# High weights against high and low input in one product of 512 columns, in 45 units of a two-block transformer kernel

## The reference

```
# first block, MLP
u = rms_norm(h, norm_mlp_pre)
f = square(relu(u @ w_mlp_in)) @ w_mlp_out            # 1024 -> 4096 -> 1024
# second block, peer_ffn: x is the normed state, 16384 experts, 8 heads, 16 picked per head
q = x @ w_query;  s1 = q[..., 0] . keys_1;  s2 = q[..., 1] . keys_2
v1, i1 = top_k(s1, 16);  v2, i2 = top_k(s2, 16)
top_score, pos = top_k(v1[:, None] + v2[None, :], 16)
gates = softmax(top_score)
act = gelu(x . expert_down[picked], approximate=False)
y = sum over picked of gates * act * expert_up[picked]
```

## Time and profile before

| | us |
|---|---|
| median of 3 runs | 1545.17 |
| lowest, highest | 1544.93, 1547.18 |
| the profiled execution, whole | 1545.45 |
| its span | 1543.6 |
| PE busy in it | 1505.9 (98%) |
| DVE, ACT, POOL busy | 1037.6, 840.9, 366.4 |

### The profile page before, as it was taken

The page is one execution under the profiler, slowest core; times in us unless marked ns, Lnnn a source line. Parts: engine busy times, 40 slices in busy tenths (PEclk is TensorE's granted clock), DMA queues, the critical chain, the costliest instruction groups (busy, mean ns, idle before and its releaser), DMA issues.

```text
span 1543.6 us, 29249 instructions
## 1 busy us (share of the span) xinstructions
PE 1505.9 (98%) x11442; PEld 1423.4 (92%) x11442; DVE 1037.6 (67%) x1813; ACT 840.9 (54%) x1648; POOL 366.4 (24%) x398
## 2 busy tenths in 40 slices
PE   7999999999889999999999999999999999999998
PEld 7888989999889999999999999999999888888887
DVE  5666666555679774687999957777774555555554
ACT  4576465444455544454444467777775544455544
POOL 1452430000437652403655520011112000000000
PEclk9999999999999999999999999999999999999999
DMA  6752555555435622455455554444445555555664
GB/s 207 229 174 90 164 169 182 186 182 184 133 107 165 194 97 96 132 184 173 146 173 170 176 192 137 140 144 141 137 139 177 194 196 195 192 191 193 195 195 139
DMA packets 76805, 255.15 MB, mean 165 GB/s; under 512 B 9359, under 2 KB 15325, under 8 KB 76541
## 3 DMA queue, kind: packets, MB, share of 16 engines
q1 hardware_dynamic: 76429, 252.63, 50.3%
q0 software_dynamic: 240, 0.66, 0.2%
HBM read 250.23 MB, written 2.75 MB: 164 GB/s over the span
## 4 chain that ended last, share of the span: by engine, by line
PE 83%; DVE 11%; ACT 2%; POOL 1%; issue 1%; DMA 1%; SPq 1%; POOLq 0%; DVEq 0%; ACTq 0%
PE bank L684 82%; DVE wl L1701 3%; DVE big L1701 2%; POOL big L2419 1%; DVE big L2262 1%; DMA raw<-in_wst 1%; DVE big L2273 1%; DVE big L1704 1%; DVE big L2269 1%; ACT big L1266 1%; ACT wh L1266 1%; DVE big L2258 1%; DVE big L2279 1%; DVE big L2266 1%; PE bank L1015 0%
## 5 line engine op out<-in xcount | busy, mean ns | idle before, releaser
L1701 DVE TENSOR_TENSOR wl<-raw,wh 128x1024 fp32r<-128x1024 f32 (+4 forms) x467 | 542.4, 1163 | 377.8 <-ACT wh L1266 377.4
L1266 ACT ACTIVATE wh<-raw 128x1024 fp32r<-128x1024 f32 (+1 forms) x467 | 489.7, 1052 | 317.6 <-PE bank L684 310.0
L684 PE MATMUL bank<-gw,wh 128*128 128x256 f32 x3504 | 647.2, 286 | 0.0
L684 PEld LDWEIGHTS bank<-gw,wh 128*128 128x128 f32 x3504 | 544.7, 192 | 0.2
L684 PE MATMUL bank<-gw,wl 128*128 128x256 f32 x1752 | 495.9, 283 | 5.1 <-POOL wl L2419 5.1
L684 PEld LDWEIGHTS bank<-gw,wl 128*128 128x128 f32 x1752 | 335.2, 191 | 6.5 <-issue 6.5
L684 PE MATMUL bank<-xw,wh 128*128 128x256 f32 x1696 | 324.0, 291 | 12.7 <-ACT wh L1266 8.2
L684 PE MATMUL bank<-wh,xw 128*128 128x512 f32 x1056 | 325.2, 389 | 0.0
L684 PEld LDWEIGHTS bank<-xw,wh 128*128 128x128 f32 x1696 | 269.2, 195 | 20.0 <-ACT wh L1266 8.5
L2419 POOL TENSOR_TENSOR wl<-raw,wh 128x384 fp32r<-128x384 f32 (+5 forms) x140 | 194.8, 1399 | 304.6 <-ACT wh L1266 304.6
L1266 ACT ACTIVATE big<-bank 128x256 f32<-128x256 f32 (+23 forms) x327 | 118.2, 372 | 251.1 <-PE bank L684 214.4
(11 more groups left out here) (141 smaller groups left out, 1115.5 us busy)
## 6 DMA issues: line engine op xcount, KB each, us to landing
raw<-in_wst SPq DMA_DIRECT2D x455, 512.0 KB, 3.7
big<-toeplitz SPq DMA_DIRECT2D x16, 128.0 KB, 5.6
raw<-in_w1k SPq DMA_DIRECT2D x4, 512.0 KB, 5.4
raw<-in_w1v SPq DMA_DIRECT2D x4, 512.0 KB, 4.0
big<-in_xT SPq DMA_DIRECT2D x4, 256.0 KB, 5.8
raw<-in_wst SPq DMA_DIRECT2D x4, 256.0 KB, 5.0
diag_in<-big SPq DMA_DIRECT2D x2, 512.0 KB, 3.4
big<-in_keys SPq DMA_DIRECT2D x1, 1024.0 KB, 5.4
```

The source lines that it names most:

```text
L684: return e.matmul(o, a, b, start=first, stop=last, skip_group_check=True)
L1266: return e.activation(o, x, f, **kw)
L1701: return e.tensor_tensor(o, a, b, f)
```

## The change

45 units (`WIDE`) are computed in another way: the 30 "in" units of the MLP from 59 on, and the 15 expert-down units 248 to 262, which stand ahead of the building of the table. `wide_products` multiplies `wh` by high and low input at once, 512 columns over both halves of the bank, and then `wl` by the high input, 256 columns onto the first half: 16 matmuls in place of 24. So the low part of the result stands in the second half and has to be added.

In an "in" unit ACT copies the second half into `HT` (where it wrote the Relu), DVE adds the first half of the bank to it, waits for its own result, and takes `max(x, 0) * x` in one operation in place of the square. In an expert-down unit ACT copies the second half into `LOWS` (a stretch of `misc`), DVE adds that onto the first half within PSUM, and then ACT takes the Gelu. The order on ACT in slot u there: the copy of unit u-1, the split of unit u+2 (which stood behind the Gelu before), the Gelu of unit u-1, the side jobs.

```diff
+WIDE = [u for u in HID.values() if u >= MLP + 2] + [u for u in range(DN + 39, DN + 54)]
...
+        lowA = steps("low_copied", [u for u in WIDE if u >= DN])
+        joined = steps("halves_joined", WIDE)
...
+            if u in WIDE and u < XA:
+                return joined.at(u)
             return evD.at(u) if u in evD.value else evA.at(u)
...
+                def wide_products(u, x):
+                    wh, wl = WH[:, u % RW, :], WL[:, u % RW, :]
+                    o = banks[bank_of(u)]
+                    bank_ready(u)
+                    e.wait_ge(*hi.at(u))
+                    for k in range(8):
+                        c = half(k)
+                        mm(o[:, :], wh[:, c], x[:, k, :], k == 0, k == 7)
+                        if k == 0:
+                            lo_ready(u)
+                        z = mm(o[:, 0:T], wl[:, c], x[:, k, 0:T], False, k == 7)
+                        if k == 7:
+                            z.then_inc(*unit.sent(u))
+                        if k % 2:
+                            yield
...
                         if n >= 3:
                             e.wait_ge(*hD.at(n - 3))
-                        act(HT[n % 3], ps, AF.Relu).then_inc(*evA.sent(u))
+                        if u in WIDE:
+                            act(HT[n % 3], b[:, T:2 * T], AF.Copy).then_inc(*evA.sent(u))
+                        else:
+                            act(HT[n % 3], ps, AF.Relu).then_inc(*evA.sent(u))
...
-                        e.wait_ge(*unit.at(u))
+                        if u in WIDE:
+                            e.wait_ge(*joined.at(u))
+                        else:
+                            e.wait_ge(*unit.at(u))
...
+                def low_half(u):
+                    if u - 1 in lowA.value:
+                        e.wait_ge(*joined.at(u - 1))
+                    e.wait_ge(*unit.at(u))
+                    act(LOWS, banks[bank_of(u)][:, T:2 * T], AF.Copy).then_inc(*lowA.sent(u))
...
+                    if u - 1 in lowA.value:
+                        low_half(u - 1)
+                        split(due(u))
                     if u not in HELD:
                         catch_up(s, u in FLUSH)
...
+                    elif u in WIDE and u < XA:
+                        n = MLP_UNITS[u - MLP][1]
+                        x = HT[n % 3]
+                        e.wait_ge(*evA.at(u))
+                        tt(x, ps, x, ALU.add).then_inc(*joined.sent(u))
+                        e.wait_ge(*joined.at(u))
+                        stt(x, x, 0.0, x, ALU.max, ALU.mult).then_inc(*rqD.sent(n))
+                    elif u in WIDE:
+                        e.wait_ge(*lowA.at(u))
+                        tt(ps, ps, LOWS, ALU.add).then_inc(*joined.sent(u))
```

More of the change, by code:

```diff
@@ L181, in program @@
         TG = misc[:, 1156:1412]
+        LOWS = TG
         cols = sb("cols", [128, I["cols"].shape[1]], F32)
@@ L898, in stage @@
                         return expert_up(u)
+                    if u in WIDE:
+                        return wide_products(u, XW if u < XA else GW)
                     b = banks[bank_of(u)]
```

## The result

The changed kernel takes 1548.99 us (median of 13 runs, 1546.46 to 1553.67) where the kernel before takes 1545.87 in runs on the same chip. The ratio is 1.0022, with a 95% interval of 1.0013 to 1.0031: slower by 3.1 us between the medians, where no change was forecast. Its profiled execution took 1549.84 us and its span is 1548.0 in place of 1543.6.

A forecast was written before the change was run, and what follows sets the result against it. PE, busy 98% of the span, was taken as the bound. From the profiled 1545.45 us, -3.1 + 2.5 - 0.9 + 1.4 = -0.1 gave 1545.35, or 1545.1 allowing for the runs' median 0.28 lower; range 1540.2 to 1546.8.

The forecast's parts named there:

- The products: Wide units on PE: each block loses one matmul's fixed 13.5 ns, 108 ns a unit; -3.1 us MLP, -0.9 units 255 to 262.
- the full value: Saving on PE over all 45 units, taken at its upper bound of 4.86 us; the lower bound was nothing.
- The cover in the MLP: DVE's extra 0.5 us per MLP "in" unit is hidden while PE stays busy; uncovered up to 15 us.
- The chain: End of top-k: exponential 2.37 us late behind Gelu and table load, PE waits 3.0 us at the transposes; +2.5 us.
- rival D: Expert-down units: POOL draws DVE's additions out to 1.16 us, +1.4 over the forecast, 1546.6 us; chance 0.07.
- Rival C: End of top-k: no chain delays PE, so every unit pays, -4.7 us, 1540.4; chance 0.20.
- The clock behind it: Behind PE's wait at the top-k transposes the granted clock falls; +1.4 us, bounds 0 and 1.7.
- rival B: Top-k transposes: same chain, but the clock stays at 2.4 GHz; -1.5 us, 1543.7; chance 0.27.
- The clock at the turn: PE's waits between MLP and second block: no term forecast; a 1.23 us wait was read with clock 1.00.
- Rival E: Matmul pairs on PE: long plus short take as long as three short, nothing gained, +4.0 us, 1549.2; chance 0.06.

The follow-up runs named there:

- grouped: The changed kernel with each wide unit's eight 512-column products ahead of its eight 256-column ones; 1546.91 us, ratio 1.0010 to the kernel before.
- exp_first: The changed kernel with ACT taking the top-k exponential ahead of the Gelu that waits for DVE's addition; 1545.33 us, ratio 1.0000 to the kernel before.
- warm_wait: The changed kernel with ten unread matmuls filling PE's wait for the top-k reductions; 1547.48 us, ratio 1.0006 to the kernel before.
- mlp_pad: Wide products in the MLP alone, plus seven matmuls of ones ahead of the turn behind it; 1545.50 us, ratio 0.9996 to the kernel before.
- halves: The changed kernel with each 512-column product made of two of 256; 1549.10 us, ratio 1.0024 to the kernel before.
- the expert-down half: The kernel before with wide products in the 15 expert-down units alone; 1549.27 us, ratio 1.0021 to the kernel before.
- mlp_only: The kernel before with wide products in the 30 MLP units alone; 1545.36 us, ratio 0.9996 to the kernel before.
- mlp_half: The kernel before with wide products in only the last 16 of the MLP's 30 units; 1545.97 us, ratio 0.9995 to the kernel before.

## Why the prediction was wrong

**The products: mechanism right, size wrong.** The term was 30 x 0.108 - 0.1 = -3.1 us for the MLP and -0.9 for units 255 to 262. A pair took 353 ns and not 345, so the terms are -1.6 (measured in the stretch from turn 1 to the spread; 240 pairs by 6 ns are 1.4) and -0.4 (8 units of 8 pairs by 6 ns, an estimate). The 0.1 us that PE was to wait at the start of the MLP doesn't show: its timeline has no wait from 219 to 300. The step that failed is the choice of the full value from two stages: the long matmul was read where the weights are the moving operand, and next to others of its kind. The neighbours matter by grouped, 5 ns a pair; the other 4 ns are the difference to the stage that was read, of which the moving operand is one. The prediction had set the bounds there, and then took the upper one. The Trainium skill, TensorE: Matmul & The Clock Gate, "Wait — 56ns, not 53.3ns?", gives a start-to-start time of columns over 2.4 GHz plus about 2.5 ns, 215.7 ns for 512 columns. No row here agrees: 225.7, 230 and 235 ns.

**The cover in the MLP: right.** PE is busy all 100 us from 300 to 400, DVE 63%.

**The chain: right, almost to the row.** The exponential was to be 2.37 us later and was 2.35; the split of 255 was to be 2.62 later and was 2.62; POOL's wait was to end at 887.5 and ended at 888.50 less 1.03. DVE's additions into PSUM took 0.42 us beside POOL, and weren't drawn out, so rival D falls. The wait was put at 3.0 us and measured 2.30: half of the difference is that DVE's `wl` of 255 took 0.82 us in place of 1.17, so the transposes came 2.28 us late in place of 2.62; the other half is PE, which was ready at 895.07 - 1.03 = 894.04 in place of 893.7. Rival C, that there was no chain, falls with exp_first: it is there, and it hangs on one instruction's place. The Trainium skill, ScalarE: Activation LUTs, "What ACT_TABLE_LOAD costs", gives a load of about 1.28 us, with which the trace agrees (889.41, 1.28 us), and a drain of 1.38 us on top, which it doesn't show: the exponential starts at 890.71, 0.02 us behind the load.

**The clock behind it: right.** +1.4 us forecast, 1.7 read from the windows, 1.45 between the profiles of the changed kernel and warm_wait; rival B falls for the changed kernel, and holds for the versions in which the wait is 0.91 us or filled.

**The clock at the turn: missing.** No term stood for a stretch in which no instruction was changed. The prediction had even read the first wait there, 1.23 us with a clock of 1.00, and used it as the one example of a wait that does no harm. The same wait was followed by a fall in the changed kernel, and the wait of 1.08 us behind it, which the prediction didn't read, by the fall that cost 1.55 us. One row that shows no fall says that none need follow, not that none will. The term at nothing measures about 1 us by the ratios and 1.5 in the profiles.

**The sum.** -1.6 - 0.4 + 2.3 + 1.5 and 1 to 1.5 for the turn give +2.8 to +3.3 us, for a measured 3.1 between the medians and 3.4 by the ratio. The measured 1548.99 is 3.9 above the forecast of 1545.1; the other 0.7 is that the kernel before has its median at 1545.87 in that comparison and not at 1545.17. Rival E gave nearly this time, 1549.2, with another mechanism: it had a pair saving nothing, and "slower" only below 2.7 ns a pair. A pair saves 6; the turn's clock made up for it. The range ended at 1546.8 because both errors, the choice of the upper end for the products and the missing term, lie on the same side, and the range had counted the first only as E, and not as values between. (Its ends lie 0.2 us outside the times that the prediction itself gives for C and D, 1540.4 and 1546.6.)

## What to carry to other kernels

Take the time of a matmul from rows with the same moving operand and the same neighbours, and where there are none, put the forecast between the bounds and not on the better one. Where an addition is put ahead of an activation, look for a table load in the same slot: with the load and the exponential ahead of the activation that waits, and not behind it, the loss of this change was gone. When a wait of PE can't be avoided, a few matmuls of ones in it can keep the clock, as they did at both places here; what is saved elsewhere may be given back at such a place, though nothing there was changed. And a fall of the clock has a price only where PE doesn't wait for another engine soon after: compare the time between two waits, not the clock alone.

## What the runs showed of the hardware

- fp32r matmuls with the input as moving operand, start to start at the full clock: 119 ns for 256 columns; 230 ns for 512 columns in a row, 235 when they alternate with those of 256. The stage with weights moving has 225.7; what makes the difference wasn't found.
- A wait of 2.3 us of PE was followed by 3.4 us at 1.2 GHz in 898 to 902, and cost 1.45 us besides the wait. Ten matmuls of 128 columns in that wait, or a wait of 0.91 us in its place, and the clock stayed at 2.4 GHz.
- The same wait of 1.23 us was followed by a clock that stayed at 1.00 over the next 2 us and more when it ended 193.30 to 193.98 us behind turn 1 (mlp_pad, before, halves, the expert-down half), and by a fall when it ended after 191.36 to 193.01 (grouped, mlp_only, the changed kernel, mlp_half). With one profile of each, it is a pattern and no proof.
- Some 3 us at 1.2 GHz at the turn cost nothing where a wait for POOL followed (12.66 us from wait to wait, 12.67 without it), and 1.5 us where none did (19.58 in place of 18.02).
- A DVE addition of 128x256 with a PSUM operand took 0.41 to 0.43 us with POOL at work or not; beside POOL's two 128x512 operations a subtraction of 128x640 in SBUF took 1.58 us in the changed kernel, against 0.82 without POOL at work.
